# A two-layer hybrid decoder trunk: narrow matmuls packed into parts of TensorE's array, norms of q as softmax scales, and fills and waits placed anew

## The reference, cut to what matters

```python
h = rms_norm(x, norm_g[l])
p = h @ w_in[l]
z, p_rw, p_ml, p_mla, p_da = _split(p, IN_WIDTHS)
...
y = jnp.concatenate([beta[0] * y_rw, beta[1] * y_ml, beta[2] * y_mla, beta[3] * y_da], axis=-1)
y = y * jax.nn.silu(z)
x = x + y @ w_out[l]
```

```python
# MLA: 128 columns without and 64 with rotation; the norm goes over all 192
q = rms_norm(q, q_g); k = rms_norm(k, k_g)          # q, k: (T, 4, 192)
q = jnp.concatenate([q[..., :MLA_NOPE], apply_rope(q[..., MLA_NOPE:], cos, sin)], -1)
k = jnp.concatenate([k[..., :MLA_NOPE], apply_rope(k[..., MLA_NOPE:], cos, sin)], -1)
...
# DA: two maps a head, the second subtracted with weight lam
q = rms_norm(q.reshape(B, T, DA_HEADS, 2, DA_QK), q_g)
...
s = jnp.einsum('bqhmd,bkhmd->bhmqk', q_blk, kf) * scale
p = jax.nn.softmax(where(causal, s, neg), axis=-1)
attn = jnp.einsum('m,bhmqk->bhqk', coeffs, p)
```

## Time and profile before

| | |
|---|---|
| three runs, us | 2631.59, 2634.35, 2634.81 (median 2634.35) |
| profiled execution, us | 2631.67; span 2630.0 |
| TensorE matmuls | 2491.1 us, 95% of the span |
| POOL, VectorE, ScalarE | 1730.6 (66%), 1181.4 (45%), 640.1 us (24%) |
| mean granted TensorE clock | 0.979 |
| DMA | mean 110 GB/s |

### The profile page before, as it was taken

How to read it: one execution, slowest core, us unless ns; L and a number is a source line. 1 busy time by engine, 2 the same in 40 slices (tenths; PEclk the granted TensorE clock), 3 DMA queues, 4 the chain that set the end, 5 groups by cost and what they waited for, 6 DMA issues and landing times. The chain is left out here.

```text
span 2630.0 us, 39931 instructions
## 1 busy us (share of the span) xinstructions
PE 2491.1 (95%) x16064; PEld 1853.5 (70%) x16064; DVE 1181.4 (45%) x1650; ACT 640.1 (24%) x1109; POOL 1730.6 (66%) x1196
## 2 busy tenths in 40 slices
PE   5999999999999998999969999999999999988999
PEld 4866577777777776667858666777777777766677
DVE  4123236646555762344241222366476557633442
ACT  4222211212111122332232223112122112223322
POOL 2675578658558876677626655777576588766675
PEclk9999999999999998999979999999999999999999
DMA  6622243223224335522336232432232244355223
GB/s 204 183 80 81 80 129 117 77 78 105 78 70 140 116 117 177 168 77 68 119 87 181 80 96 61 149 102 82 70 108 78 69 140 131 103 178 170 77 67 121
DMA packets 158690, 290.18 MB, mean 110 GB/s; under 512 B 21648, under 2 KB 30224, under 8 KB 156896
## 3 DMA queue, kind: packets, MB, share of 16 engines
q1 hardware_dynamic: 108864, 187.09, 25.5%
q10 hardware_dynamic: 49632, 100.46, 10.8%
HBM read 235.57 MB, written 56.10 MB: 111 GB/s over the span
## 5 line engine op out<-in xcount | busy, mean ns | idle before, releaser
L735 POOL TENSOR_SCALAR w_hi<-raw 128x512 fp32r<-128x512 f32 x552 | 899.4, 1629 | 659.2 <-PE ps_proj L765 547.4
L740 POOL TENSOR_TENSOR w_lo<-raw,w_hi 128x512 fp32r<-128x512 f32 (+1 forms) x640 | 842.1, 1316 | 224.7 <-ACT w_hi L1186 178.5
L765 PE MATMUL ps_proj<-h_hi,w_hi 128*128 128x512 f32 x1760 | 730.9, 415 | 18.2 <-POOL w_lo L740 11.1
L765 PE MATMUL ps_proj<-h_hi,w_lo 128*128 128x512 f32 x1760 | 690.7, 392 | 0.0
L765 PE MATMUL ps_proj<-h_lo,w_hi 128*128 128x512 f32 x1760 | 689.4, 392 | 0.0
L765 PEld LDWEIGHTS ps_proj<-h_hi,w_hi 128*128 128x128 f32 x1760 | 332.5, 189 | 125.2 <-issue 31.4
L765 PEld LDWEIGHTS ps_proj<-h_lo,w_hi 128*128 128x128 f32 x1760 | 333.1, 189 | 71.9 <-issue 11.1
L765 PEld LDWEIGHTS ps_proj<-h_hi,w_lo 128*128 128x128 f32 x1760 | 332.3, 189 | 72.5
L780 PE MATMUL ps_proj<-w_hi,h_hi 128*128 128x512 f32 x448 | 184.8, 412 | 3.7 <-issue 3.7
L780 PE MATMUL ps_proj<-w_lo,h_hi 128*128 128x512 f32 x448 | 177.3, 396 | 0.0
L780 PE MATMUL ps_proj<-w_hi,h_lo 128*128 128x512 f32 x448 | 177.1, 395 | 0.0
(11 more groups left out here) (332 smaller groups left out, 3208.7 us busy)
## 6 DMA issues: line engine op xcount, KB each, us to landing
raw<-in_w_in_dram SPq DMA_DIRECT2D x480, 256.0 KB, 2.7
raw<-in_w_out_dram SPq DMA_DIRECT2D x128, 256.0 KB, 3.0
projected<-stage ACTq DMA_DIRECT2D x118, 256.0 KB, 2.9
arena<-projected ACTq DMA_DIRECT2D x90, 256.0 KB, 3.1
arena<-out_dram ACTq DMA_DIRECT2D x2, 4096.0 KB, 16.6
gated_hi<-arena ACTq DMA_DIRECT2D x24, 256.0 KB, 2.3
gated_lo<-arena ACTq DMA_DIRECT2D x24, 256.0 KB, 2.9
h_hi<-gated_hi SPq DMA_DIRECT2D x8, 768.0 KB, 6.8
```

The source lines that it names most:

```text
L735: nc.gpsimd.tensor_scalar(hi, src, 1.0, None, ALU.mult).then_inc(s_hi_split, 1)
L740: nc.gpsimd.tensor_tensor(lo, src, hi.bitcast(F32), ALU.subtract).then_inc(s_raw_split, 1)
L765: last = mm(ps_proj[:, m, :], lhsT, rhs, start=(k == 0 and j == 0), stop=(k == KT - 1 and j == 2))
```

## The change

It does the following.

- **Gates.** The i and f columns (4 + 4) lie in a piece of 32; its high part and its low part stand side by side in one operand of 64 columns, so that the tile takes two matmuls instead of three. The two parts are loaded as two lanes and added by DVE.
- **MLA.** The rotated columns of two heads are made by one set of three matmuls with 128 columns, in every second head. Constants and per-column gains stand twice over the partitions. DVE adds the rotated rows' squares to the others' (half of the k part's square to each), so that k's sum is one matmul; q's sum is four matmuls with one column each, and its root isn't multiplied into q, but becomes the scale of the softmax's Exp and of the row maxima. The rotation is two matmuls in two quarters of the array.
- **DA.** q's sums become matmuls with two columns and its roots the scale of Exp; the scores of both maps stand next to each other, and the two masks behind them.
- **RW and ML.** The third lora product moves to rows 64 to 95. The f row's product of ML reads four rows from 64, brought there by a DMA. The gates' Exp and Ln move from ahead of RW's v copy to the end of head pair 1.
- **Start of a layer.** The lam product, its Exp and its DVE part move into the MLA stage; the small operations on the parameters stand ahead of DVE's wait for the mean; a high part of a weight follows each of the first four parts of h.
- **DA stage.** On ACT the fill `to_z_da` stands ahead of `square_qk(0)`. Each part of y is loaded as soon as its steps allow, from step 253 of the loads on, where it was 265.
- **Table.** The numbers in `FILL` change, with the total of tiles the same.

```diff
-    + [[(MLA0 + 512, P + 64), (RW0 + 3 * G, 64), (ML0 + 4 * G, P)]]
+    + [[(MLA0 + 512, P + 64), (RW0 + 3 * G, 64), (ML0 + 4 * G, LANE)]]
...
+Y_LOADS = STEPS - KT + 3 + N_RAW + N_SPLIT
...
-    da_first=4, da_sums=(16, 11, 11, 11), da_scores=(8, 5, 5, 5), da_half=(14, 12, 12, 12), da_turned=(0, 3, 3, 3),
-    da_osq=(0, 9, 3, 3), da_gate=(8, 14, 14, 14))
+    ml_first=27, ml_qk=(17, 10, 10, 10), ml_s=(8, 7, 7, 6), ml_h=(14, 14, 12, 11), ml_gate=(12, 12, 12, 12),
+    da_first=17, da_sums=(16, 10, 10, 10), da_scores=(8, 6, 6, 6), da_half=(13, 15, 18, 18), da_turned=(3, 3, 3, 3),
+    da_osq=(3, 4, 3, 3), da_gate=(9, 10, 10, 10))
...
+                        rows = slice(0, P)
+                        if g == G_MISC and m == 2:
+                            both = w1[:, 2 * P:2 * P + 2 * LANE]
+                            rows, products = slice(0, 2 * LANE), ((both, h1), (both, h2))
...
-                    pe.wait_ge(s_lam_ready, 1)
-                    mm(ps_proj[:, 1, 0:2], ones[0:64, :], lam_prod[0:64, :], start=True, stop=True
-                       ).then_inc(s_da_lam_mm, 1)
...
-                        for j in range(3):
-                            mm(ps[0:64, 1, :], la_wq[:, j, q0 + P:q0 + 192], la_in[:, j, :],
-                               start=(j == 0), stop=(j == 2))
+                            mm(ps[:, 0, :], la_wq[:, j, h * P:(h + 1) * P], la_in[:, j, :], start=(j == 0), stop=(j == 2))
+                        own = slice(64 * (h % 2), 64 * (h % 2) + 64)
+                        if h % 2 == 0:
+                            for j in range(3):
+                                mm(ps[:, 1, :], la_wq_pe[:, j, h * 64:h * 64 + P], la_in[:, j, :], start=(j == 0), stop=(j == 2))
...
-                        mm(ps[:, 3, :], ones, la_hsq[:, 0, :], start=True, stop=False)
-                        mm(ps[:, 3, :], ones[0:64, :], la_hsq[0:64, 1, :], start=False, stop=True)
-                        mm(ps[:, 0, :], ones, la_hsq[:, 2, :], start=True, stop=False)
-                        mm(ps[:, 0, :], ones[0:64, :], la_pesq[0:64, :], start=False, stop=True)
-                        mm(ps[0:64, 1, :], rot_mla[0:64, :], la_qp[0:64, :], start=True, stop=True
-                           ).then_inc(s_la_heads_sums, 1)
+                        pe.wait_ge(s_la_squared, 2 * h + 2)
+                        mm(ps[:, 0, :], ones, la_hsq[:, 2, :], start=True, stop=True)
+                        pe.wait_ge(s_la_squared, 2 * h + 3)
+                        for i in range(NT):
+                            qs = slice(i * P, (i + 1) * P)
+                            last = mm(ps[:, 3, i:i + 1], la_hsq[:, 0, qs], ones[:, 0:1], start=True, stop=True)
+                        last.then_inc(s_la_sums, 1)
+                        if h % 2 == 0:
+                            for half in (slice(0, 64), slice(64, P)):
+                                last = mm(ps[half, 1, :], rot_mla[half, :], la_qp[half, :], start=True, stop=True)
+                            last.then_inc(s_la_turned_pe, 1)
...
-                        mm(ps[:, 2, :], rw_vup[0:32, cols], rw_vd[0:32, :], start=True, stop=True
+                        mm(ps[:, 2, :], rw_vup[64:96, cols], rw_vd[64:96, :], start=True, stop=True
...
-                        mm(ps[:, 1, :], sel_f[0:36, h * P:(h + 1) * P], ml_gt[0:36, :], start=True, stop=True
+                        mm(ps[:, 1, :], sel_f[64:68, h * P:(h + 1) * P], ml_gt[64:68, :], start=True, stop=True
...
                                     mm(ps[:, b, ks], da_g[half, 0, qs], da_g[half, 1, ks], start=True, stop=False)
-                                    last = mm(ps[:, b, qs], mask_ident, neg, start=False, stop=True)
+                                for m in range(2):
+                                    last = mm(ps[:, 2 * (i % 2) + m, qs], mask_ident, neg, start=False, stop=True)
...
-                        if k == 3:
-                            for n in range(N_SPLIT):
-                                high_part(n)
+                        if k < N_SPLIT:
+                            high_part(k)
...
-                            nc.scalar.activation(la_p[:, i, 0:(i + 1) * P], ps[:, i, 0:(i + 1) * P], ACT.Exp, scale=192.0 ** -0.5, bias=la_mx[:, i:i + 1], accum_out=la_sum[:, i:i + 1]).then_inc(s_probs_exp, 1)
+                            nc.scalar.activation(la_p[:, i, 0:(i + 1) * P], ps[:, i, 0:(i + 1) * P], ACT.Exp, scale=la_rq[:, i:i + 1], bias=la_mx[:, i:i + 1], accum_out=la_sum[:, i:i + 1]).then_inc(s_probs_exp, 1)
...
-                        if hp == 1:
-                            act.wait_ge(s_ml_gate_abs, 1)
-                            link(nc.scalar.activation(ml_sg[32:36, :], ml_sg[32:36, :], ACT.Exp, scale=-1.0))
-                            nc.scalar.activation(ml_sg[32:36, :], ml_sg[32:36, :], ACT.Ln, bias=1.0).then_inc(s_ml_gate_log, 1)
...
+                    fill("to_z_da")
                     square_qk(0)
-                    fill("to_z_da")
...
+                        dve.wait_ge(s_la_head_squared, 2 * h + 1)
+                        v.tensor_tensor(la_hsq[:, 2, :], la_hsq[:, 2, :], la_pesq, ADD).then_inc(s_la_squared, 1)
+                        dve.wait_ge(s_la_head_squared, 2 * h + 2)
+                        v.tensor_tensor(la_hsq[own, 0, :], la_hsq[own, 0, :], la_hsq[own, 1, :], ADD).then_inc(s_la_squared, 1)
```

More of the change, by code:

```diff
@@ L170, in rotation @@
         return m
-    put("rot_mla", rotation(64, 32, 64))
+    put("rot_mla", np.concatenate([rotation(64, 32, 64)] * 2))
     put("rot_da", rotation(P, 8, 64))
@@ L210, in parameters @@
             table[:, layer, COLS[name]] = given[name][layer, :P]
-            table[0:64, layer, COLS[name] + 1] = given[name][layer, P:]
+            for at in (0, 64):
+                table[at:at + 64, layer, COLS[name] + 1] = given[name][layer, P:]
         for name in ("da_q_g", "da_k_g"):
@@ L763, in project @@
                             products = ((w1[:, part], h1), (w1[:, part], h2), (w2[:, part], h1))
+                        rows = slice(0, P)
+                        if g == G_MISC and m == 2:
+                            both = w1[:, 2 * P:2 * P + 2 * LANE]
+                            rows, products = slice(0, 2 * LANE), ((both, h1), (both, h2))
                         for j, (lhsT, rhs) in enumerate(products):
-                            last = mm(ps_proj[:, m, :], lhsT, rhs, start=(k == 0 and j == 0),
-                                      stop=(k == KT - 1 and j == 2))
+                            last = mm(ps_proj[rows, m, :], lhsT, rhs, start=(k == 0 and j == 0),
+                                      stop=(k == KT - 1 and j == len(products) - 1))
                         if m == tiles_of(g) - 1:
@@ L841, in _ @@
                         mm(ps[:, 1, :], ones, la_sq[:, 3 + j, :], start=(j == 0), stop=(j == 1))
-                    mm(ps[0:64, 2, :], rot_mla[0:64, :], la_peg[0:64, :], start=True, stop=True
-                       ).then_inc(s_la_sums, 1)
+                    for half in (slice(0, 64), slice(64, P)):
+                        last = mm(ps[half, 2, :], rot_mla[half, :], la_peg[half, :], start=True, stop=True)
+                    last.then_inc(s_la_sums, 1)
+                    pe.wait_ge(s_lam_ready, 1)
+                    mm(ps[:, 3, 0:2], ones[0:64, :], lam_prod[0:64, :], start=True, stop=True
+                       ).then_inc(s_da_lam_mm, 1)
                     fill("la_sums")
-                    pe.wait_ge(s_la_latents, 1)
+                    pe.wait_ge(s_la_scaled, 1)
+                    pe.wait_ge(s_da_lam_exp, 1)
                     for i in range(NT):
@@ L909, in _ @@
                     for j in range(4):
-                        last = mm(ps[0:32, 0, :], rw_vdn[:, j, :], rw_v[:, j, 1:T + 1], start=(j == 0), stop=(j == 3))
+                        last = mm(ps[64:96, 0, :], rw_vdn[:, j, :], rw_v[:, j, 1:T + 1], start=(j == 0), stop=(j == 3))
                     last.then_inc(s_rw_vdn_mm, 1)
@@ L1111, in _ @@
                         pe.wait_ge(s_da_squared, h + 1)
-                        mm(ps[:, 0, :], bones, da_sq[:, 0, :], start=True, stop=True)
                         mm(ps[:, 1, :], bones, da_sq[:, 1, :], start=True, stop=True)
+                        for i in range(NT):
+                            last = mm(ps[:, 0, 2 * i:2 * i + 2], da_sq[:, 0, i * P:(i + 1) * P], bones[:, 0:P:64], start=True, stop=True)
+                        last.then_inc(s_da_sums, 1)
                         mm(ps[:, 2, :], rot_da, da_g[:, 0, :], start=True, stop=True)
-                        mm(ps[:, 3, :], rot_da, da_g[:, 1, :], start=True, stop=True).then_inc(s_da_sums, 1)
+                        mm(ps[:, 3, :], rot_da, da_g[:, 1, :], start=True, stop=True).then_inc(s_da_rotated, 1)
                         fill("da_sums", h)
@@ L1176, in evacuate @@
                             act.wait_ge(s_stored[m], 16 * (g - (m == 3 and g > G_MISC)))
```

(5 more changed lines are left out.)

176 lines of the change are left out of this document (102 added, 74 removed).

## The result

The changed kernel takes 2509.36 us, median of four runs (2502.68 to 2513.98), beside 2634.58 for the kernel before: ratio 0.953, 95% interval 0.9509 to 0.9551, that is 125 us less, where 2491 was forecast in a range of 2460 to 2535.

What follows compares the result with a forecast made beforehand. TensorE's in-order queue, with matmuls for 2491 of 2630 us, was taken as the bound. Work -61, waits -61 and clock -20 made -142 from 2631.67, so 2490, forecast as median 2491, range 2460 to 2535 (own range 2465 to 2515).

Steps and rivals of the forecast that it cites:

- Work of TensorE: Cheaper matmuls in MLA, DA, RW lora, gates and mLSTM, with small costs added: -61 us in sum.
- DA scores: In DA heads, neighbouring products of the two halves overlap, so a head costs 3.7 us instead of 7.1: -27 us.
- u and f: mLSTM products of 36 and 4 rows in two shapes: +1.6 us, between -7 if overlapped and +2 if not.
- The gates: Gates tile, three full products become two of 64 columns, with two changes of shape: +5 us, or -7 if changes are free.
- Start of a layer: Turns no longer wait for lam and the first w_hi part follows the first h part: -15.4 us over both layers.
- DA: Waits counted to the DA stage, 43 us in all, shrink to some 3 a layer: -37 us, range -25 to -40.
- MLA and mLSTM: Waits: MLA's evacuation tile and small waits -6 us; mLSTM's wait at L1079 and smaller ones -4 us.
- RW: L946's waits go, -5.5 us a layer, but evacuations ahead of tanh give back +5.3 a layer: net +1.3 us.
- Clock: Half-clock stretches behind the shortened waits go or shrink: -20 us of a possible 36, range -10 to -30.
- That the pairs don't overlap: Rival: 64-row fp32 product pairs do not overlap, +22 us for DA, +7 lora, +4 rotation: 2524 us; chance 0.1.
- That the chains don't get shorter: Rival: DVE and ACT chains in MLA and DA heads stay long, +35 to 40 us: 2528 us; chance 0.2.
- The clock did not fall through the heads: Rival: TensorE runs at 1.2 GHz through the 16 MLA and DA heads, +330 us less 142; chance 0.04.

Runs made afterwards that it cites:

- experiment 1: Changed kernel with each DA mask product put back directly behind its own map's product, so the two maps' products are not neighbours: 2531.32 us.
- experiment 2: Changed kernel with the mLSTM f row's product reading 36 rows from row 64 (zeros added) instead of 4: 2497.99 us.
- experiment 8: Changed kernel with the four high parts of weights in one piece again behind the fourth part of h: 2513.9 us.
- experiment 5: Changed kernel with ACT's evacuations ahead of the kept-y wait and mLSTM loads, and x asked for behind the first q and k preparation: 2493.66 us.
- experiment 10: Changed kernel with the edits of experiments 2, 4 and 5, constants asked for ahead of q and k, three tiles more in two places: 2468.47 us.
- experiment 12: Kernel of experiment 10 with seven tiles moved from ahead of the first mLSTM head into RWKV head pairs 1 to 3: 2473.52 us.
- Experiment 3: Changed kernel with ACT's tanh of z ahead of the four evacuations at the end of RWKV head pair 1: median 2506.85 us.
- experiment 9: Kernel of experiment 10 with the 4 MB copy of x to the output asked for later, by ACT's queue behind its squares: 2477.01 us.
- experiment 11: Kernel of experiment 10 with four tiles moved from the factors of RWKV head pair 1 to its lora products: 2464.28 us.
- experiment 6: Changed kernel's code with the table of fills of the kernel before: 2551.8 us.
- experiment 4: Changed kernel with tanh and the gates' Exp and Ln ahead of head pair 1's evacuations, DVE's gate operations behind head pair 2's squares: 2499.64 us.

## Why the prediction was right, and where it missed

The forecast was 142 us less, the profiled execution had 118: work came out 14 better, waits 18 and the clock 20 worse. The mechanisms of the work term held and were shown; that the total lies well inside the range owes something to luck, since the gates' miss (12 us, see below) made up for two thirds of what the waits lacked. Two of the prediction's own signs went against it. Waits were to stay under 80 us in all, and the list has 88.7; the clock was to be 0.985, and was 0.981. There is also a slip in the last step: 2631.67 - 142 + 2.7 is 2492, not 2491.

**Work of TensorE, forecast -61, measured -75.** By start-to-start times, summed over each group's instructions at full clock: MLA products -13.0 (forecast -13), MLA sums -23 (-22), DA scores 7.0 to 3.6 a head, -27 (-27), lora -7 (-7), u and f +1.6 (+1.6), narrow sums and lam +1 (+1). The gates were the miss: "two changes of shape, +0.38 by the earlier trace rows: +5"; it was -7. The step that failed took the price of a change between 64 and 128 rows in fp32 for one between 64 and 128 columns in fp32r. The two differ in the type and in what is cut, and no run took them apart, so that it stays open which of them carries the price; in MLA's fp32 products a change of columns alone did cost something, 0.15 us over three. The rule of the Trainium skill ("TensorEngine Tiling (Array Packing)", Tiling Modes), that a change of mode drains TensorE, holds here for the u and f products, which didn't overlap, and is not to be seen at the gates, where two changes cost 0.02 us together. That tiles of one mode work independently, which the same section says, agrees with experiments 1 and 2: 1.37 and 2.23 us for the halves of a DA head, and 0.01 us between the starts of u and f.

**Waits, forecast -61, measured -43.**
Start of a layer: -12 for -15.4, -3.9 in layer 1 (33.65 to 29.75) and -8.1 in layer 2. "The first w_hi part follows the first h part, which takes 3.4 us out before POOL" held in layer 2, by experiment 8; in layer 1 the weight was not there.
DA: -31 for -37, from 43 to 11 (L1136 4.7, L800 3.9, L878 2.8). L1177, L859 and the loads of y went as forecast. The step that was short is the one that costed nothing for the constants: `da_const` is asked for behind the kept y, and TensorE, with less to do ahead of it, waits 2.7 and 2.0 us. By experiment 5 x is not the main cause; in experiment 10, asked for a little earlier and with three tiles more, the wait is gone, and which of the two did it stays open.
MLA and mLSTM: forecast -6 and -4, measured +1 and +2; this is the largest miss among the waits. The wait of 2.2 us for an evacuation went, but L917 and L883 came up, 3.6 and 2.1, and the tile ahead of the first mLSTM head, 6.7. I had looked at which waits a fill covers and not at where each group's end comes to stand relative to ACT, which waits for the kept y there; experiment 5 shows it, and experiment 12 makes the same wait again from the other side.
RW: +1.3 forecast, about -3 measured (29.0 to 25.7 us by the rows of the two lists, those without a releaser with them). L942's wait in head pair 2 was 4.5, as forecast, from ACT's four evacuations ahead of tanh:

```profile
582.62 0.60 ACT L1205 ACTIVATE stage<-ps_proj 128x512 f32<-128x512 f32 x1 [4.28 <-PE ps_proj L785]
...
586.84 0.63 ACT L1236 ACTIVATE arena<-arena 128x512 f32<-128x512 f32 x1 [0.46 <-ACT stage L1205]
```

and L946's two waits went. But behind L942 the wait for the squares did not come: TensorE was late itself, so that RW came out 4 to 5 us better.

**Clock, forecast -20, measured nothing in the profiled execution.** Half clock still held 95 us. The windows over these stretches hold as much matmul work as before, 77.8 us after 77.0; what went was idle time in them:

```profile
sum 94.20, PE 77.78 PEld 50.50 DVE 39.80 ACT 33.64 POOL 18.84; mean PE 5.19 PEld 3.37 DVE 2.65 ACT 2.24 POOL 1.26
```

The step that failed is that the stretches behind the shortened waits would go with them. Most stretches began at a wait, but not every wait is followed by one: L917's 1.8 us at 189 was not, and the same wait at 1433 had 13.7 us of half clock behind it, in which TensorE never paused, as this window of the changed kernel shows:

```profile
1434.90:1448.60 13.70, 13.70 (x27) 6.75 (x27) 2.35 (x7) 2.51 (x8) 1.10 (x2) 0.50 0.08 20
```

The changed kernel's four runs had clocks of 0.981, 0.981, 0.984 and 0.983 and times of 2514, 2512, 2503 and 2506. Experiment 3 left the waits as they were (89.5 us) and had 0.987 in its profiled execution and 2497.65, and 2506.85 as its median. So some 10 us lie in the clock's own scatter, half of the forecast's 20. The highest clocks, 0.988 to 0.993, are those of the kernels of experiments 9 to 12, which have 71 to 80 us in their lists; but among them the one with least waiting (71.3, experiment 10) has the lowest, 0.988, so that how much a wait costs in clock stays open.

**The rivals.** That the pairs don't overlap fell with the timeline and experiment 1. Its -5 for the saved changes of shape was priced too low: six changes a head at 0.16 to 0.19 us, by rows 6, make 8 to 9. Experiment 1 would then have been 8 to 9 us slower, and it was 22. That the chains don't get shorter was half right: with the old table (experiment 6) the waits for DA's halves grew to 19.2 us and 42 us of the gain were gone; the new table covered that, and the forecast's -37 doesn't show how much of the table is needed only to stand still. The clock did not fall through the heads; it stayed at half for 95 us in all.

## What to carry to other kernels

Two fp32 products on separate rows of the array overlapped here when they were neighbours in the queue and had the same shape, and did not with a mask between them or with 36 rows beside 4; pad the smaller with zeros to get it, and put what belongs to both (a mask) behind the pair. When matmuls that cover another engine's chain get cheaper, the covering work must be placed anew in the same change: here that was a third of the gain. After each such shift look where the group ends fall on the evacuating engine, and try a moved wait on the chip, because in experiments 3, 4, 11 and 12 the wait came back, in part or whole, at another link of the chain or at an evacuation; in 5 and 10 it stayed away.

## What the runs showed that I had not expected

A product with 64 columns in fp32r stands between ones of 128 for 0.02 us, so that a high and a low part of 32 columns each can share one operand, and a tile takes two products (0.47 us) instead of three (0.68). Thirty-two more rows, of zeros, made the u and f pair cost 1.05 us instead of 2.11. Executions of the changed kernel differ by 11 us, with clocks of 0.981 to 0.984. And a 4 MB copy asked for 11 us later and in another queue made the first projection matmul start 4.4 us later, with the DMA engines at 1.05 of their time in that window.
